# Two half-height matmul pairs in the array: index scores and recurrent gate products on rows 0-63 and 64-127, gate tanh in four pieces

## The chip, the core and the metric

The kernel runs on one core of a Trainium2 chip. The core has a matrix engine (TensorE, PE in the profile, its weight loads PEld), a vector engine (VectorE, DVE), an activation engine (ScalarE, ACT), a general engine (GpSimd, POOL) and a queue engine (SyncE, SP). They run side by side and meet at semaphores. The metric is the device time of one execution in microseconds, the median of several; lower is better.

## What is computed

Two transformer-like blocks run one after the other on 512 tokens of width 1024. Only the first block is touched. Cut to what matters:

```python
u = rms_norm(x, norm1_w) @ w_in                      # split into rnn_x, rnn_gate, q, k, v, iq, ik, iw, g
xc = causal_depthwise_conv(rnn_x, conv_w, conv_b)
r = sigmoid(block_diag_linear(xc, wa, ba))           # 16 blocks of 64 x 64
i = sigmoid(block_diag_linear(xc, wx, bx))
log_a = -8 * r * softplus(-lam); a = exp(log_a)
h = scan(a, sqrt(-expm1(2 * log_a)) * (i * xc))      # recurrence over the tokens
y_rnn = h * gelu(rnn_gate)
rel = relu(einsum('bqhd,bsd->bqhs', iq, ik))         # 8 index heads of 64 channels
score = einsum('bqhs,bqh->bqs', rel, iw) * scale     # its 128 largest per query row are kept
# sparse attention over the kept keys, two output projections, gates, then a feed-forward block
```

After that the first block's feed-forward part follows, and a second block with a gated linear attention, a sliding-window attention, a cross attention and a convolved feed-forward part.

## The kernel before, in words

All activations lie with the channels on the 128 partitions and the 512 tokens along the row. A "job" is one 128-channel output tile of a projection: 8 weight tiles, each with three matmuls (lines 314 to 316: high times high, high times low, low times high part), so 24 matmuls of 512 columns into one PSUM bank. The weights stream in through `raw` (SyncE queue), ScalarE makes the high part (`split`, line 794), GpSimd the low part (line 286), and TensorE takes the job. VectorE takes the result out of PSUM with `take` (a `tensor_tensor` at line 1320). Each engine's order is written out by hand; semaphores carry the dependences.

**Index scores.** The 512 tokens are 4 tiles of 128; for tiles 1 to 3 and 8 heads there are 24 products, of 256, 384 and 512 columns (line 393). Two heads of 64 channels share one 128-partition tile of `p1`. The key tile `ikz` has two copies: `ikz[:, 0]` holds the key in partitions 0-63 and zeros below, `ikz[:, 1]` zeros above and the key in partitions 64-127, so each product runs over all 128 rows and the zeros drop the other head. The zeros are written by a VectorE memset (line 1382). Each product goes to one of three PSUM banks `s_ps[n % 3]`; ScalarE applies relu (line 866) into one of two buffers, and VectorE multiplies by the head's weight and adds (lines 1317 and 1324). TensorE waits before product n for relu n-3, ScalarE before relu n for sum n-2.

**Recurrent part.** Four pairs of tiles (u = 0 and 1), by a loop of three and one pair more (`rnn_pair` on ScalarE and VectorE, `rnn_body` on TensorE). For each tile VectorE finishes the convolution (`conv_tail`), TensorE makes two gate products from it (`rnn_gates`, line 430), over all 128 rows, with a block-diagonal 128 x 128 weight for each gate, into one bank each, and one semaphore step after the second. ScalarE's `rnn_decay` then takes a tanh of each bank (lines 909 and 910), waits for them, and takes an exp and a second tanh (lines 912 and 913). TensorE's order in one round of the loop is: two jobs, gates of tile 0, a job, gates of tile 1, a job. ScalarE's order is: head of the convolution (line 898) and a square (line 903) for each tile, two splits, `rnn_decay(0)`, a split, `rnn_decay(1)`, two tanh for the gelu (line 947), a split, two square roots, two copies to `b_hi`. In the last pair the three later jobs and splits are absent. VectorE uses the two decays one after the other, then the scan (line 1493).

Where names in rows need a word: "score" and "o" are PSUM banks, "job" the two job banks, "turn" the banks `t_ps`, "arena" the large SBUF tile that holds `p1`, `ikz`, `rc`, `rr`, `ri` and most others.

## Time and profile before

| | us |
|---|---|
| median of 3 runs (1743.75 to 1743.93) | 1743.75 |
| the profiled execution | 1743.67 |
| its span, from first to last instruction | 1741.6 |
| TensorE busy in it | 1659.6 |
| VectorE, ScalarE, GpSimd busy | 727.8, 693.1, 791.0 |
| index products on TensorE | 60.0 to 76.4 |
| VectorE's top-128 search | 95.3 to 154.8 |
| recurrent part, first to last gate product | 172.2 to 269.0 |

The 1741.6 us of the span and the 2.1 us around it make the 1743.67 us. The profile shows for each engine what it did, when, and what its idle time ended with. "Idle before" with an arrow names what came last. A product in plain 32-bit format stands in the profile as two matmul records, so "x24" in index rows is 12 products, and a gate visit of two products is four records. The granted clock (PEclk) is the share of the full TensorE clock: 1.00 is 2.4 GHz, 0.50 is 1.2 GHz.

### The profile page before, as it was taken

To read this page: it belongs to the slowest core of one execution; us is meant where nothing else is said; L and a number is where in the kernel's file an instruction comes from. 1 tells how busy PE (TensorE), PEld (TensorE's weight loads), DVE (VectorE), ACT (ScalarE), POOL (GpSimd) and SP (SyncE) were. 2 spreads that over 40 slices of the span, in tenths; PEclk is the share of its full clock that TensorE was granted. 3 is DMA by queue.
4 is the path that set the end of the run, shared out by engine and by line. 5 is a ranking of instruction groups with operands and counts; after the bars stand their busy time and mean duration, and the time that the engine had idled before them with its cause. 6 is when DMAs were issued, how large, how long until landed. Compare 5 with 4: busy or idle time off the path is not lost.

```text
span 1741.6 us, 23147 instructions
## 1 busy us (share of the span) xinstructions
PE 1659.6 (95%) x7686; PEld 1350.5 (78%) x7686; DVE 727.8 (42%) x1343; ACT 693.1 (40%) x1127; POOL 791.0 (45%) x1060
## 2 busy tenths in 40 slices
PE   6999986999999999999999999789999999999997
PEld 5787764777788888888888888678986888888886
DVE  5487886545323321212123532633223453353354
ACT  5322655544333432323233423843354443243242
POOL 5334442222355454545455541035843456456453
PEclk9999998999999999999999999999999999999998
DMA  5122221111222323223233222013421233223221
GB/s 184 59 73 81 76 72 49 49 49 46 99 97 97 97 97 97 97 96 96 96 105 97 73 88 70 1 61 121 143 88 49 85 103 103 92 96 102 94 96 64
DMA packets 45100, 149.64 MB, mean 86 GB/s; under 512 B 4648, under 2 KB 7856, under 8 KB 45040
## 3 DMA queue, kind: packets, MB, share of 16 engines
q1 hardware_dynamic: 38016, 138.43, 24.3%
q10 hardware_dynamic: 7024, 10.41, 1.7%
q8 instruction: 38, 0.62, 0.1%
q14 instruction: 22, 0.18, 0.0%
HBM read 146.58 MB, written 2.11 MB: 85 GB/s over the span
## 4 chain that ended last, share of the span: by engine, by line
PE 86%; DVE 9%; ACT 3%; issue 2%; ACTq 0%; DVEq 0%
PE job L314 24%; PE job L316 24%; PE job L315 24%; DVE arena L1317 2%; PE o L486 2%; PE score L456 2%; DVE arena L1426 1%; DVE small L1423 1%; DVE arena L1320 1%; PE score L393 1%; PE score L430 1%; PE score L714 1%; DVE arena L1493 1%; PE job L746 1%; PE turn L355 1%
## 5 line engine op out<-in xcount | busy, mean ns | idle before, releaser
L286 POOL TENSOR_TENSOR w_lo<-w_raw,w_hi 128x256 fp32r<-128x256 f32 x1056 | 790.8, 781 | 924.5 <-ACT w_hi L794 923.8
L314 PE MATMUL job<-a_hi,w_hi 128*128 128x512 f32 (+1 forms) x1120 | 432.9, 387 | 16.5 <-POOL w_lo L286 9.8
L316 PE MATMUL job<-a_hi,w_lo 128*128 128x512 f32 (+1 forms) x1120 | 424.7, 379 | 0.0
L315 PE MATMUL job<-a_lo,w_hi 128*128 128x512 f32 (+1 forms) x1120 | 424.5, 379 | 0.0
L794 ACT ACTIVATE w_hi<-w_raw 128x1024 fp32r<-128x1024 f32 x264 | 275.2, 1050 | 282.8 <-PE job L316 273.0
L314 PE MATMUL job<-b_hi,w_hi 128*128 128x512 f32 x952 | 374.9, 394 | 0.0
L316 PE MATMUL job<-b_hi,w_lo 128*128 128x512 f32 x952 | 371.0, 390 | 0.0
L315 PE MATMUL job<-b_lo,w_hi 128*128 128x512 f32 x952 | 370.4, 389 | 0.0
L314 PEld LDWEIGHTS job<-a_hi,w_hi 128*128 128x128 f32 x1120 | 212.6, 190 | 59.6 <-DVE a_lo L1317 10.8
L315 PEld LDWEIGHTS job<-a_lo,w_hi 128*128 128x128 f32 x1120 | 212.6, 190 | 39.5 <-issue 2.1
L316 PEld LDWEIGHTS job<-a_hi,w_lo 128*128 128x128 f32 x1120 | 212.0, 189 | 39.8
L316 PEld LDWEIGHTS job<-b_hi,w_lo 128*128 128x128 f32 x952 | 178.7, 188 | 37.7
L314 PEld LDWEIGHTS job<-b_hi,w_hi 128*128 128x128 f32 x952 | 178.8, 188 | 36.6 <-issue 0.2
L315 PEld LDWEIGHTS job<-b_lo,w_hi 128*128 128x128 f32 x952 | 178.9, 188 | 36.0 <-issue 0.2
L1320 DVE TENSOR_TENSOR arena<-arena,job 128x512 f32<-128x512 f32 (+1 forms) x80 | 55.0, 688 | 274.1 <-PE job L316 274.1
L1320 DVE TENSOR_TENSOR arena<-job,rstd 128x512 f32<-128x512 f32 (+1 forms) x117 | 80.1, 688 | 188.1 <-PE job L316 160.4
L1317 DVE SCALAR_TENSOR_TENSOR arena<-arena,vec 128x512 f32<-128x512 f32 x112 | 98.7, 881 | 65.4 <-ACT arena L1267 53.0
L809 ACT ACTIVATE sq<-arena 128x512 f32<-128x512 f32 x48 | 30.2, 631 | 129.5 <-DVE arena L1320 127.2
L1320 DVE TENSOR_TENSOR a_lo<-arena,a_hi 128x512 f32 (+1 forms) x62 | 42.3, 692 | 69.8 <-ACT a_hi L1026 42.2
L1267 ACT ACTIVATE arena<-arena,vec 128x512 f32<-128x512 f32 x44 | 35.6, 808 | 87.8 <-DVE arena L1320 87.8
L1025 ACT ACTIVATE arena<-arena 128x512 f32<-128x512 f32 x32 | 20.2, 632 | 106.5 <-DVE arena L1317 106.5
L1317 DVE SCALAR_TENSOR_TENSOR arena<-job,rstd 128x512 f32<-128x512 f32 x32 | 22.1, 692 | 91.2 <-PE job L316 86.6
(255 smaller groups left out, 1386.7 us busy)
## 6 DMA issues: line engine op xcount, KB each, us to landing
w_raw<-w_all SPq DMA_DIRECT2D x264, 512.0 KB, 3.3
arena<-x_t ACTq DMA_DIRECT2D x8, 512.0 KB, 6.0
out_t<-arena ACTq DMA_DIRECT2D x8, 256.0 KB, 2.1
arena<-rg_w ACTq DMA_DIRECT2D x4, 256.0 KB, 2.7
arena<-row_table ACTq DMA_DIRECT2D x1, 1024.0 KB, 5.2
arena<-mem_t ACTq DMA_DIRECT2D x1, 1024.0 KB, 6.6
arena<-consts ACTq DMA_DIRECT2D x1, 384.0 KB, 3.7
cst<-consts ACTq DMA_DIRECT2D x1, 260.0 KB, 8.1
```

The source lines that it names most:

```text
L286: nc.gpsimd.tensor_tensor(w_lo[:, sl, c], raw[:, sl, c], w_hi[:, sl, c].bitcast(F32), ALU.subtract).then_inc(s("lo_ready"), 1)
L314: mm(ps[:, 0:n], w_hi[:, sl, c], hi[:, kt, 0:n], start=kt == 0, stop=False)
L315: mm(ps[:, 0:n], w_hi[:, sl, c], lo[:, kt, 0:n], start=False, stop=False)
L316: ins = mm(ps[:, 0:n], w_lo[:, sl, c], hi[:, kt, 0:n], start=False, stop=kt == last)
L456: mm(ps, q_now[:, u, qt * P:qt * P + P], kz[:, 2 * kvt + half, 0:w], start=True, stop=True).then_inc(s("att_mm"), 1)
L486: ins = mm(o_ps[:, kt * P:T], vz[:, 2 * kvt + half, kt, :], prob_t[:, kt, kt * P:T], start=half == 0 and kt == 0, stop=half == 1 and kt == ...
L794: fn(w_hi[:, sl], raw[:, sl], ACT.Copy).then_inc(s("hi_ready"), 1)
L809: fn(sq[:, f % 2, :], src, ACT.Square).then_inc(s("sq_ready"), 1)
L1025: fn(act_s[:, c % 2, :], act_t[:, c % 2, :], ACT.Square).then_inc(s("ff_sq"), 1)
L1267: fn(f_c[u], f_u[u][:, PAD:PAD + T], ACT.Identity, scale=vcol("conv_w2", col + 88), bias=vcol("conv_b2", col)).then_inc(s("f_head"), 1)
L1317: return v.scalar_tensor_tensor(out=out_, in0=a, scalar=sc, in1=b, op0=op0, op1=op1)
L1320: return v.tensor_tensor(out_, a, b, op)
```

## The change

- The second key copy moves into the same row as the first: `ik_rows` holds the key in partitions 0-63 and again in 64-127, with no zeros. Head h uses rows 0-63 or 64-127 of both operands, so two consecutive products stand on different halves of the array's rows. The memset of `ikz` is gone.
- The two gate products of a tile work on rows 0-63 and on rows 64-127. The weight tile is 128 x 128 and holds both gates: the first product's bank has gate a of the even block in partitions 0-63 and gate x of the even block in 64-127; the second product's bank has gate x of the odd block in 0-63 and gate a of the odd block in 64-127. The load of these weights is half as large.
- So each tanh reads two banks. It becomes four activations of 64 partitions x 512, two of which read one half of the partitions and write the other.

```diff
-        ikz = tiles(30, 2)
+        ik_rows = arena[:, 30, :]
...
-        rgw = tiles(30, 2)[:, :, 0:2 * P]
+        rgw = tiles(30, 2)[:, :, 0:P]
...
-                mm(s_ps[n % 3][:, 0:P * (t + 1)], p1[:, J_IQ + h // 2, t * P:t * P + P],
-                   ikz[:, h % 2, 0:P * (t + 1)], start=True, stop=True).then_inc(s("idx_mm"), 1)
+                r = slice(64 * (h % 2), 64 * (h % 2) + 64)
+                mm(s_ps[n % 3][:, 0:P * (t + 1)], p1[r, J_IQ + h // 2, t * P:t * P + P],
+                   ik_rows[r, 0:P * (t + 1)], start=True, stop=True).then_inc(s("idx_mm"), 1)
...
                 for c in range(2):
-                    ins = mm(rnn_ps[u][c][:], rgw[:, u, c * P:c * P + P], rc[u], start=True, stop=True)
+                    r = slice(64 * c, 64 * c + 64)
+                    ins = mm(rnn_ps[u][c][:], rgw[r, u, :], rc[u][r, :], start=True, stop=True)
...
-            act.dma_start(ikz[64:128, 1, :], ikz[0:64, 0, :]).then_inc(s("ik_landed"), 16)
+            act.dma_start(ik_rows[64:128, :], ik_rows[0:64, :]).then_inc(s("ik_landed"), 16)
...
-                fn(rr[u], rnn_ps[u][0][:], ACT.Tanh, scale=0.5, bias=half_ba_at(f)).then_inc(s("act_step"), 1)
-                fn(ri[u], rnn_ps[u][1][:], ACT.Tanh, scale=0.5, bias=half_bx_at(f)).then_inc(s("rnn_tanh"), 1)
+                even, odd = slice(0, 64), slice(64, 128)
+                fn(rr[u][even], rnn_ps[u][0][even], ACT.Tanh, scale=0.5, bias=half_ba_at(f)[even]).then_inc(s("act_step"), 1)
+                fn(rr[u][odd], rnn_ps[u][1][odd], ACT.Tanh, scale=0.5, bias=half_ba_at(f)[odd]).then_inc(s("act_step"), 1)
+                fn(ri[u][even], rnn_ps[u][0][odd], ACT.Tanh, scale=0.5, bias=half_bx_at(f)[even]).then_inc(s("act_step"), 1)
+                fn(ri[u][odd], rnn_ps[u][1][even], ACT.Tanh, scale=0.5, bias=half_bx_at(f)[odd]).then_inc(s("rnn_tanh"), 1)
...
-            did(v.memset(ikz, 0.0))
...
-            stt(ikz[0:64, 0, :], p1[0:64, 0, :], vcol("ikn")[0:64], t_ps[0][0:64, :]).then_inc(s("ik_normed"), 1)
+            stt(ik_rows[0:64, :], p1[0:64, 0, :], vcol("ikn")[0:64], t_ps[0][0:64, :]).then_inc(s("ik_normed"), 1)
...
-    rg_w = np.zeros((8, P, 2 * P), f32)
+    rg_w = np.zeros((8, P, P), f32)
...
-        rg_w[n // 2, r, P + 64 * (n % 2):P + 64 * (n % 2) + 64] = wx[n]
+        rg_w[n // 2, r, 64 - 64 * (n % 2):P - 64 * (n % 2)] = wx[n]
```

On VectorE, early in the program, between the set-up of the small columns and the first norm. Before:

```order
L1320 TENSOR_TENSOR small<-vec 128x1
L1380 MEMSET arena 128x2048
L1381 MEMSET arena 128x2048
L1382 MEMSET arena 128x1024
L1339 RECIPROCAL rcol<-rcol 128x4
L1320 TENSOR_TENSOR arena<-job,rstd 128x512 x2
```

And now:

```order
L1325 TENSOR_TENSOR small<-vec 128x1
L1385 MEMSET arena 128x2048
L1386 MEMSET arena 128x2048
L1344 RECIPROCAL rcol<-rcol 128x4
L1325 TENSOR_TENSOR arena<-job,rstd 128x512 x2
```

The third memset is gone; the reciprocal, for which TensorE waits with the spread of the norm (line 355), follows the second.

On ScalarE, `rnn_decay(1)` of the loop: it begins after the split of line 794 and is followed by the gelu's tanh. Before:

```order
L794 ACTIVATE w_hi<-w_raw 128x1024
L908 REGISTER_ALU
L909 REGISTER_ALU
L909 ACTIVATE arena<-score,small 128x512
L910 REGISTER_ALU
L910 ACTIVATE arena<-o,small 128x512
L912 ISA
L912 ACTIVATE arena<-arena,small 128x512
```

And now:

```order
L796 ACTIVATE w_hi<-w_raw 128x1024
L910 REGISTER_ALU
L912 REGISTER_ALU
L912 ACTIVATE arena<-score,small 64x512
L913 ISA
L913 ACTIVATE arena<-o,small 64x512
L914 REGISTER_ALU
L914 ACTIVATE arena<-score,small 64x512
L915 ISA
L915 ACTIVATE arena<-o,small 64x512
L917 ISA
L917 ACTIVATE arena<-arena,small 128x512
```

Nothing moved past anything else; two activations stand where one stood, twice. TensorE has the same instructions in the same order, with 64 instead of 128 rows at lines 393 and 430 (now 394 and 432).

## Rows read from the trace of the kernel before

**Rows 1.** The head of the page.

```profile
span 1741.6 us, 23147 instructions
```

**Rows 2.** Chain of waits at 28 to 34 us: start us, us, what.

```profile
31.81 0.16 issue
31.98 0.91 DVE arena L1382
32.89 0.05 DVE rcol L1339
```

**Rows 3.** Timeline of TensorE: start us, us, what, [idle before <-releaser].

```profile
32.98 1.16 PE L355 MATMUL turn<-cst,rcol 128*128 128x128 f32 x8 [1.51 <-DVE rcol L1339]
```

**Rows 4.** Timeline of VectorE and of ScalarE in the index stage.

```profile
72.06 5.89 DVE L1317 SCALAR_TENSOR_TENSOR arena<-arena,small 128x512 f32<-128x512 f32 x7 [0.24 <-ACT arena L866]
...
76.43 0.60 ACT L866 ACTIVATE arena<-score 128x512 f32<-128x512 f32 x1 [0.26 <-PE score L393]
```

**Rows 5.** Timeline of VectorE after the index stage.

```profile
102.82 0.69 DVE L1320 TENSOR_TENSOR arena<-job,rstd 128x512 f32<-128x512 f32 x1 [1.12 <-PE job L316]
...
158.79 1.29 DVE L1320 TENSOR_TENSOR arena<-job,rstd 128x512 f32<-128x512 f32 x2
```

**Rows 6.** Stretches: busy (count) of PE, PEld, DVE, ACT, POOL, clock, DMA share, GB/s.

```profile
156.60:159.50 2.90, 0.15 (x1) 0.00 (x0) 2.81 (x8) 0.00 (x0) 2.69 (x4) 0.98 0.56 181
159.40:162.80 3.40, 3.26 (x8) 2.58 (x9) 2.53 (x5) 2.28 (x3) 0.76 (x1) 0.50 0.49 154
...
1111.70:1115.00 3.30, 3.30 (x17) 3.30 (x17) 0.90 (x4) 2.98 (x12) 0.00 (x0) 0.50 0.00 0
1120.10:1123.00 2.90, 0.15 (x1) 0.00 (x0) 1.31 (x6) 2.90 (x11) 0.00 (x0) 1.00 0.00 0
...
1142.40:1145.70 3.30, 3.30 (x10) 2.57 (x9) 2.95 (x5) 2.60 (x5) 0.62 (x1) 0.51 0.00 0
```

**Rows 7.** Timeline of TensorE around the gate products of the second pair.

```profile
200.47 3.61 PE L430 MATMUL score<-arena 128*128 128x512 f32 x4 [2.94 <-DVE arena L1317]
...
209.39 1.02 PE L430 MATMUL score<-arena 128*128 128x512 f32 x2
210.24 1.02 PE L430 MATMUL o<-arena 128*128 128x512 f32 x2
```

**Rows 8.** Timeline of ScalarE, second pair and last pair.

```profile
204.18 1.28 ACT L909 ACT_TABLE_LOAD   x1 [0.78 <-PE score L430]
205.47 0.69 ACT L909 ACTIVATE arena<-score,small 128x512 f32<-128x512 f32 x1
206.06 0.68 ACT L910 ACTIVATE arena<-score,small 128x512 f32<-128x512 f32 x1
...
208.32 1.04 ACT L794 ACTIVATE w_hi<-w_raw 128x1024 fp32r<-128x1024 f32 x1
211.39 0.69 ACT L909 ACTIVATE arena<-score,small 128x512 f32<-128x512 f32 x1 [2.03 <-PE o L430]
...
267.07 0.80 ACT L913 ACTIVATE arena<-arena,small 128x512 f32<-128x512 f32 x1
269.19 0.69 ACT L909 ACTIVATE arena<-score,small 128x512 f32<-128x512 f32 x1 [1.32 <-PE o L430]
```

**Rows 9.** Timeline of TensorE where half-height products stand already (line 581).

```profile
1023.51 1.05 PE L564 MATMUL score<-arena 128*128 128x128 f32 x8
1024.49 1.71 PE L581 MATMUL turn<-arena 64*128 64x128 f32 x16
1026.13 0.50 PE L314 MATMUL job<-b_hi,w_hi 128*128 128x512 f32 x1
1026.46 0.40 PE L315 MATMUL job<-b_lo,w_hi 128*128 128x512 f32 x1
```

**Rows 10.** The products of line 581 in two short stretches: length, PE busy (count touched).

```profile
1024.90:1024.93 0.03, 0.03 (x3) 0.03 (x2) 1.00 0.00 0
1025.29:1025.32 0.03, 0.03 (x5) 0.03 (x4) 1.00 0.00 0
```

## Prediction, made before the changed kernel ran

> **What bounds the kernel now.** I read the page first, then the chain of waits, then the timelines of the touched stages, then stretches with the granted clock. The span is 1741.6 us [rows 1], the profiled execution 1743.67, the median 1743.75; the sum below is made against 1743.67 and the difference of 0.08 is ignored. Most of the chain is TensorE's job matmuls, which the change leaves alone, so what counts is the first 286 us. The chain there goes: VectorE's memsets at 30 to 33 us, then TensorE without a pause to 102.6 (the index products are part of it), then VectorE's top-128 search to 158.8, then TensorE's jobs, then four rounds in which it passes through TensorE, ScalarE and VectorE in turn. A gain on TensorE in the index stage reaches the end, since VectorE idles 1.12 us at 102.82 for a job of TensorE's; later in the search it is VectorE alone, which then starts earlier by the same amount [rows 5]. After 286 us everything only moves, unless the clock changes.
>
> **1. The memset of the zero rows.** It takes 0.91 us and stands right ahead of the reciprocal that TensorE waits for [rows 2]. TensorE has idled 1.51 us by then [rows 3], so the cover ends 0.6 us beyond the gain. Gain: 0.91 us, all on the path. Lower bound 0.8 (the issue gap of 0.16 may stay), upper 1.07.
>
> **2. Index products.** Does TensorE overlap products on different row halves? The trace has such products at line 581: 4 products (8 records) on one half, then 8 records on the other. In a slice where one half runs 3 records are in flight, in the slice where the second has begun there are 5 [rows 10]. So yes. The same rows price the change of array shape. The 8 records of line 564 take 0.98 us to the next start; at 0.11 each they need 0.89, so entering costs 0.09. On leaving, the first job matmul takes 0.33 us (1026.13 to 1026.46) instead of 0.23 [rows 9]. With the first half-height weight load not hidden and the drain on the way out, both estimates of mine at 0.1, entering and leaving cost about 0.2 each.
>
> But this stage is mostly VectorE's. In the last third it spends 5.89 us on 7 sums, 0.84 each, idling 0.24 before them; TensorE needs 0.86 for a product of 512 columns (two records of 0.43), and relu waits 0.26 for it [rows 4]. With overlap TensorE drops out and VectorE's 0.84 sets the pace, so the sums end only 0.2 to 0.6 us earlier. TensorE gains more: its last product may start when relu 20 is done, which follows sum 18, five sums before the end: 5 x 0.84 = 4.2 us before the last sum ends, then 0.1 + 0.60 for relu, 0.1, and 0.86 for the product: it ends 2.5 us before the last sum. Before, the last relu starts at 76.43, so the product ended at 76.4, and the last sum ended at 77.95: 1.5 us before. That is 1.0 us earlier, plus 0.2 for VectorE's idling, minus 0.2 for leaving. I take 0.95 us (0.4 to 1.3). The waits stay where they are; queued behind them on TensorE is the V job, which nothing else holds.
>
> **3. Gate products.** At full clock a visit is 4 records of 0.43 = 1.71 us (209.39 to about 211.1); after an idle of 2.94 us the clock is 1.2 GHz and each record takes about 0.86 [rows 7]. Overlapped, a visit takes 0.86 + 0.05 for the second start + 0.2 to enter = 1.1, and 0.2 is lost on leaving. At half clock it is 1.7 + 0.2 against 3.6.
>
> **4. Tanh in four pieces.** No half-height activation stands in the trace. Bounds: an activation's time goes by its columns, so 64 x 512 costs 0.59 us from start to start (205.47 to 206.06), like 128 x 512; at worst it is a full 0.69 with no overlap of successive ones [rows 8]. At the other end, if half the height were half the work, nothing is added. I take 0.59, since all 512 columns remain: two more pieces, +1.18 us per tile (0 to +1.6), 9.4 us of ScalarE time in all. Only what of it lies on the chain counts:
>
> - Pair 0 (no idle ahead, full clock): tile 1's tanh starts when TensorE has done visit, job, visit. Gain 1.71 - 1.3 = 0.4 for the first, 0.6 for the second, against +1.18: **+0.15**.
> - Pairs 1 and 2: ScalarE is free at 203.40 (0.78 before 204.18). Then table load 1.28, the pieces to the end of the split (205.47 to 209.36, 3.89), plus 1.18: tile 1 may start at 209.8 instead of 211.39. ScalarE's idle of 2.03 us is thus used up [rows 8]. TensorE: the first visit is 1.65 shorter, of which the job gives back about half as more of it falls in the low clock, and the second is 0.6 shorter: also about 209.8. So -1.5 + 1.18 = **-0.35** each. ScalarE holds it there even if the clock were full, so the clock matters little here.
> - Pair 3: only 1.32 us of ScalarE's time is idle before tile 1 (267.87 to 269.19). The first tile's two extra pieces use 1.18 of it, so tile 1 starts just 0.15 earlier, however fast TensorE is, and then pays 1.18: **+1.05**.
>
> Sum: 0.15 - 0.7 + 1.05 = +0.5 us. The halved weight load was not waited for: 0. Moving halves across partitions: 0.
>
> A rule of the Trainium skill speaks against this part: TensorEngine Tiling (Array Packing), section Performance Considerations, warns that tiling speeds up TensorE but not the emptying of PSUM, which may become the bottleneck. Taken alone it would say that all eight tiles pay, +9.4 us; the rows of ScalarE's idle time say that three pairs of four hide most of it. The page's section Tiling Modes says that a change of mode drains the array; rows 9 agree, at about 0.1 us for the gap that is seen.
>
> **5. The clock.** TensorE idles at 156.6 to 159.5 and then runs at half clock for 3.4 us, which costs 1.7 us in the jobs that lead to the first gates. Idles of such a length don't always do this: 1120.1 to 1123.0 has the same length, at full clock, and no row shows a fall at it [rows 6]. What decides is where an idle falls, and parts 1 and 2 move this one by 1.86 us. I give 0.55 that the fall goes, 0.45 that it stays. The jobs after it have their weights ready, so the whole 1.7 us would be gained. Later falls, as at 1111.7 and 1142.4 [rows 6], cost 1.2 to 1.7 us each and may also go, and a new one may appear.
>
> **The sum.** -0.9 - 0.95 - 1.7 + 0.5 = -3.05 us: 1743.67 - 3.05 = 1740.6; with a little for a new fall I forecast **1740.8 us**.
>
> **The rivals.**
> - *A, forecast*: the fall at 159.4 goes, others about as before: 1740.8. Chance 0.40; its own range 1739.5 to 1742.
> - *B, the fall stays*, all else as summed: 1743.67 - 1.35 = 1742.3 (up to 1744 if the index gain is at its lower bound). Chance 0.22.
> - *C, the shift also takes one to three later falls away* (1.2 to 1.7 each): 1740.6 - 1.4 to - 4 = 1736.6 to 1739.2. For it: several falls follow idles of 2 to 3 us whose place counts, and nothing reserves their place. Against: some idles that have no fall may get one. Chance 0.28.
> - *D, slower: the gate halves do not overlap.* At line 581 overlap began only after several records of one half; a gate visit has two records a half. If the second half waits for the first, a visit costs 1.71 + 0.4 instead of 1.1 + 0.2. Tile 1 of pairs 0 to 2 then starts 0.8 us later than before, not 1.0 to 1.5 earlier, and pays 1.18: +2.0 x 3, pair 3 +1.5, index gain about 0: 1743.67 + 7.5 - 0.9 = 1750.3. It makes the kernel slower by more than what can be told once pairs 0 to 2 lose over 1.0 us each. Chance 0.06.
> - *E, the pieces cost 0.69 or more apiece* without pipelining across banks and halves: +0.4 for each tile, so +0.8 a pair: A and B become 1744 to 1745.5. Chance 0.04.
> - *The change does not do what it says* (the halves of the index do not overlap, VectorE keeps its pace anyway): part 2 gives 0: inside B.
>
> **How the numbers follow.** A measurement of this kernel can tell about 0.2%, 3.5 us, from no change, so faster means below 1740.3, slower above 1747.2. C is faster wholly (0.28); of A's range about a quarter is (0.09): faster 0.37. D is slower (0.06). The rest, 0.57, is within. The range runs from inside C to E's lower end: 1737.3 to 1744.2; it leaves out D, most of E, and the lowest part of C.
>
> **What would show it.** Memset: the spread of the norm (line 355) starts at 32.1, not 32.98. Index: the V job starts about 1.9 us earlier than 76.4; VectorE's gaps in the last third are gone; the take before the first gates moves from 158.8 to 156.9. Clock: full or half at the jobs behind it. Gates: records of both halves start within 0.1 us of each other. ScalarE: pieces 0.59 apart; its idle before tile 1's pieces is near zero in all pairs but the first; in pair 3 the end of the recurrent part comes 1 us later relative to its start. Wrong if: records of a visit follow one another at 0.43; pieces take under 0.4 or over 0.65; or the falls of the clock change in the part after 300 us by more than two.

## The result: slower by 0.3%, and the profile after

The kernel after takes 1749.26 us (median of 10 runs, 1745.72 to 1752.24), the kernel before 1743.84 us (10 runs, 1742.16 to 1744.78); the ratio is 1.0029, with a 95% interval of 1.0020 to 1.0038. The forecast was 1740.8 us with a range of 1737.3 to 1744.2. The profiled execution of the kernel after took 1751.23 us; its page begins:

```profile
span 1749.4 us, 23174 instructions
```

The span was 1741.6 us before [rows 1]. The table cuts this difference at six places that both traces have; each column is what was added (+) or saved (-) in the stretch that ends there, in us. I worked it out from the start times of the instructions in the traces. The lower rows are kernels from the experiments, on the same footing: each is one execution, compared with the profiled execution of the kernel before. Behind the last column the closing norm takes up to 1.3 us more or less, with the clock that it meets, so a row does not add up to the difference of its times exactly.

| kernel | to the norm's spread (32.98) | to the V job's second matmul (76.46) | to the last top-k step (154.04) | to the first attention turn (285.94) | to the last score product of the next stage (963.22) | to the last job matmul (1726.30) | time of this execution |
|---|---|---|---|---|---|---|---|
| after | -0.84 | +0.09 | 0.0 | **+3.27** | +0.83 | **+4.19** | 1751.23 |
| after, profiled again | -0.90 | -0.16 | 0.0 | +4.03 | +0.96 | +2.31 | 1748.91 |
| index part alone | -0.75 | -0.16 | 0.0 | -0.05 | +0.01 | +1.23 | 1742.68 |
| gate part alone | +0.44 | +0.02 | 0.0 | +3.16 | +0.82 | +2.03 | 1749.17 |
| four pieces, full-height products | +0.45 | +0.01 | 0.0 | +7.37 | +1.28 | -1.71 | 1751.45 |
| half-height products, two tanh | +0.22 | +0.02 | 0.0 | -5.12 | +1.07 | -1.49 | 1738.83 |
| memset moved | -1.02 | +0.04 | 0.0 | -1.18 | +1.30 | -1.65 | 1741.41 |
| memset moved, early signal | +0.25 | -0.08 | 0.0 | -3.14 | +1.13 | -1.54 | 1740.62 |

So the change loses in two places: the recurrent part (154 to 286 us), which holds the gate products and the tanh, and the time behind 963 us, where none of its instructions runs. The first column also holds what differs between executions ahead of the changed code: up to 0.45 us, and 1.3 us in the last row, where TensorE stands at half clock to 32.4 us and the spread waits for TensorE's own jobs. The recurrent part, too, differs between executions where its code is the same: -0.05 (index part alone), -1.18 (memset moved; the fall of the clock at 231.1 us is missing there), and +3.27 against +4.03 in the two of the kernel after.

**The start.** TensorE's timeline in the kernel after (start us, us, what, [idle before <-releaser]):

```profile
32.14 1.16 PE L355 MATMUL turn<-cst,rcol 128*128 128x128 f32 x8 [0.40 <-DVE rcol L1344]
```

The same row stood at 32.98 with 1.51 us of idle [rows 3]. From the start of VectorE's first memset to its reciprocal it is now 3.83 us (28.14 to 31.97) instead of 4.90 (27.91 to 32.81); 0.23 us of the 1.07 are lost to a later start in this execution. The gain of 0.84 us lies within the forecast's 0.8 to 1.07.

**The index stage.** VectorE's sums, ScalarE's last relu and the first V job matmuls of the kernel after, from the timelines of the three engines:

```profile
60.53 0.35 DVE L1329 TENSOR_SCALAR arena<-arena,small 128x256 f32<-128x256 f32 x1 [0.42 <-ACT arena L868]
...
71.97 5.88 DVE L1322 SCALAR_TENSOR_TENSOR arena<-arena,small 128x512 f32<-128x512 f32 x7 [0.24 <-ACT arena L868]
...
76.24 0.60 ACT L868 ACTIVATE arena<-score 128x512 f32<-128x512 f32 x1 [0.25 <-DVE arena L1322]
...
75.37 0.50 PE L314 MATMUL job<-a_hi,w_hi 128*128 128x512 f32 x1
75.71 0.39 PE L315 MATMUL job<-a_lo,w_hi 128*128 128x512 f32 x1
```

The first sum of the stage in the kernel before, VectorE's timeline:

```profile
61.14 0.35 DVE L1324 TENSOR_SCALAR arena<-arena,small 128x256 f32<-128x256 f32 x1 [0.23 <-ACT arena L866]
```

Before, the relu waited 0.26 us for TensorE and the seven sums began at 72.06 [rows 4]. Now the relu waits 0.25 us for VectorE, and the seven sums begin at 71.97, although the first sum of the stage began 0.61 us earlier. Part of that is the fall of the clock at 64.8 us in this one execution. In the kernel with the index part alone (an experiment below), whose execution has no such fall, the rest of the loss sits at one place, the fourth sum. VectorE's timeline there:

```profile
60.61 0.35 DVE L1325 TENSOR_SCALAR arena<-arena,small 128x256 f32<-128x256 f32 x1 [0.42 <-ACT arena L867]
61.06 1.07 DVE L1318 SCALAR_TENSOR_TENSOR arena<-arena,small 128x256 f32<-128x256 f32 x2
62.67 2.84 DVE L1318 SCALAR_TENSOR_TENSOR arena<-arena,small 128x256 f32<-128x256 f32 x5 [0.53 <-DVE arena L1318]
```

The fourth sum starts 2.06 us after the first, against 1.64 in the kernel before.

**A gate visit**, TensorE's timeline:

```profile
208.64 0.69 PE L432 MATMUL score<-arena 64*128 64x512 f32 x1
208.65 0.69 PE L432 MATMUL o<-arena 64*128 64x512 f32 x1
209.17 0.59 PE L432 MATMUL score<-arena 64*128 64x512 f32 x1
209.18 0.59 PE L432 MATMUL o<-arena 64*128 64x512 f32 x1
209.70 0.50 PE L314 MATMUL job<-a_hi,w_hi 128*128 128x512 f32 x1
```

The two job matmuls behind the same visit in the kernel before, whose first record starts at 209.39 [rows 7]:

```profile
210.70 0.79 PE L314 MATMUL job<-a_hi,w_hi 128*128 128x512 f32 x1
211.33 0.40 PE L315 MATMUL job<-a_lo,w_hi 128*128 128x512 f32 x1
```

Both halves start within 0.01 us of each other. From the first of them to the next job's first matmul it is 1.06 us and to its second 1.39 (210.03), against 1.31 and 1.94 before. So a visit is 0.55 us shorter, with the price of entering and leaving in it; the prediction had 0.4, or 0.6 without the price of leaving. The prediction's 1.71 is four records of 0.43, which is not the distance to the next job.

**The tanh pieces** of the second pair, ScalarE's timeline, and below them rows up to its tile 1 and two rows of the last pair:

```profile
204.60 0.69 ACT L912 ACTIVATE arena<-score,small 64x512 f32<-64x512 f32 x1
205.32 0.69 ACT L913 ACTIVATE arena<-score,small 64x512 f32<-64x512 f32 x1
206.03 0.69 ACT L914 ACTIVATE arena<-score,small 64x512 f32<-64x512 f32 x1
206.74 0.68 ACT L915 ACTIVATE arena<-score,small 64x512 f32<-64x512 f32 x1
207.57 0.82 ACT L917 ACTIVATE arena<-arena,small 128x512 f32<-128x512 f32 x1
...
209.00 1.04 ACT L796 ACTIVATE w_hi<-w_raw 128x1024 fp32r<-128x1024 f32 x1
209.94 0.67 ACT L912 ACTIVATE arena<-score,small 64x512 f32<-64x512 f32 x1
...
269.49 0.80 ACT L918 ACTIVATE arena<-arena,small 128x512 f32<-128x512 f32 x1
270.19 0.67 ACT L912 ACTIVATE arena<-score,small 64x512 f32<-64x512 f32 x1
```

The pieces start 0.71 us apart, where the two full-height ones of before were 0.59 apart (205.47, 206.06 [rows 8]): a tile needs 2.97 us from its first tanh to its Exp. The idle of 2.03 us ahead of tile 1 is gone, as foretold: ScalarE goes from the split at 209.00 straight on. In the last pair it goes straight from L918 to the next tile.

**The clock**, in stretches of the kernel after (length, busy (count) of PE, PEld, DVE, ACT, POOL, then the granted clock, DMA share, GB/s):

```profile
64.90:68.10 3.20, 3.20 (x10) 2.27 (x10) 2.52 (x5) 2.31 (x5) 0.00 (x0) 0.50 0.00 0
160.40:163.60 3.20, 3.20 (x9) 2.49 (x8) 2.01 (x3) 0.82 (x1) 2.31 (x3) 0.50 0.30 116
...
228.70:235.30 6.60, 4.68 (x10) 2.65 (x11) 5.63 (x7) 4.30 (x6) 5.56 (x7) 0.50 0.26 74
...
1136.60:1146.70 10.10, 8.21 (x35) 7.51 (x35) 0.14 (x1) 3.80 (x10) 0.00 (x0) 0.50 0.00 0
1150.30:1153.50 3.20, 3.20 (x9) 2.52 (x8) 2.54 (x5) 2.20 (x4) 0.93 (x2) 0.50 0.00 0
```

The fall at 160 us is still there. The one at 228.7 lasts 6.8 us instead of 3.4, and the next, from 259.3 on, 17.1 instead of 6.8. At 1136.6 the clock is at 1.2 GHz for 10 us, and once more at 1150.3 for 3.4 us. The kernel before had full clock there up to its fall of 3.4 us at 1142.4 [rows 6]:

```profile
1136.60:1142.30 5.70, 2.85 (x20) 2.52 (x20) 1.86 (x4) 3.75 (x8) 0.00 (x0) 1.00 0.00 0
```

### The profile page after: what moved, and what is told of

Read it like the earlier page. It is cut to its first block, busy times and chain, and to the rows that moved or that the text cites. A ratio compares the mean times of both kernels' runs of the same rounds, so it can differ in the third digit from the quotient of the medians.

```text
span 1749.4 us, 23174 instructions
## 1 busy us (share of the span) xinstructions
PE 1661.5 (95%) x7686; PEld 1351.1 (77%) x7686; DVE 725.8 (41%) x1342; ACT 704.6 (40%) x1143; POOL 791.3 (45%) x1060
## 4 chain that ended last, share of the span: by engine, by line
PE 85%; DVE 8%; ACT 4%; issue 2%; ACTq 0%; DVEq 0%
PE job L314 24%; PE job L316 24%; PE job L315 24%; PE o L488 2%; DVE arena L1322 2%; PE score L458 2%; DVE arena L1430 1%; DVE small L1427 1%; DVE arena L1325 1%; PE score L394 1%; PE score L716 1%; DVE arena L1497 1%; PE job L748 1%; PE turn L355 1%; ACT arena L1166 1%
```

## Experiments

### The two parts apart

The first pair of kernels splits the change. The index part alone takes the half-height index products, the single `ik_rows` tile and the missing memset, and leaves the gates:

```diff
-                mm(s_ps[n % 3][:, 0:P * (t + 1)], p1[:, J_IQ + h // 2, t * P:t * P + P],
-                   ikz[:, h % 2, 0:P * (t + 1)], start=True, stop=True)
+                r = slice(64 * (h % 2), 64 * (h % 2) + 64)
+                mm(s_ps[n % 3][:, 0:P * (t + 1)], p1[r, J_IQ + h // 2, t * P:t * P + P],
+                   ik_rows[r, 0:P * (t + 1)], start=True, stop=True)
...
-            did(v.memset(ikz, 0.0))
```

> Index part of the change alone: half-height index products and no memset of zero rows; gates and tanh as before. By the sum of parts as the two traces now show them, the spread of the norm starts 0.85 us earlier, the index stage itself gives back 0.1 (its sums go at VectorE's pace), and the top-128 search ends 0.75 us earlier: 1743.8 - 0.75 = 1743.1 if nothing else moves. Theory 'half-height products count as less work for the clock': the granted clock falls inside the index stage (near 64 to 68 us) as in the changed kernel, though TensorE is busy. Rival 'it was the gates': no fall there. Theory 'alignment': the falls after 1080 us differ from before in number or length, and the total is off the 1743.1 by 1 to 4 us with nothing changed there.

Measured: 1743.2 us (median of 11, 1740.47 to 1746.3), ratio 0.9998 (0.9989 to 1.0007). In its profiled execution the start gives 0.75 us and the index stage 0.16; behind 963 us the clock takes 1.23 and, in the closing norm, gives back 1.3 (its product of line 355 at 1730.80 takes 1.16 us instead of 2.07). There is no fall of the clock at 64 to 68 us, and the falls behind 1080 us differ (6.8 us at 1134.7), as its last theory had it. The gate part alone is the rest of the change:

```diff
-                    ins = mm(rnn_ps[u][c][:], rgw[:, u, c * P:c * P + P], rc[u], start=True, stop=True)
+                    r = slice(64 * c, 64 * c + 64)
+                    ins = mm(rnn_ps[u][c][:], rgw[r, u, :], rc[u][r, :], start=True, stop=True)
```

together with the smaller weight load and the four tanh pieces.

> Gates part alone: half-height gate products, half weight load, four tanh pieces; index stage and memset as before. Theory 'pieces': ScalarE's pieces of 0.71 us from start to start cost more than TensorE's 1.1 us visits give back; the attention stage starts about 3.5 to 4 us later than before, total 1747.5 to 1748 if later falls are as before. Rival 'the index part is what hurts': total within 1.5 us of before.

Measured: 1748.8 us (5 runs, 1748.47 to 1751.06), ratio 1.0035 (1.0021 to 1.0049). It loses 3.16 us in the recurrent part, as expected (the attention starts 3.6 us later), and 2.03 behind 963 us. The loss of the kernel after comes with the gate part.

### ScalarE's price and TensorE's gain apart

The kernel before with the tanh in four half-height pieces, each reading and writing the same rows, over full-height products (the cuts from here on leave out the signals at the ends of some lines, and this one the two lines that are replaced):

```diff
+                fn(rr[u][even], rnn_ps[u][0][even], ACT.Tanh, scale=0.5, bias=half_ba_at(f)[even])
+                fn(rr[u][odd], rnn_ps[u][0][odd], ACT.Tanh, scale=0.5, bias=half_ba_at(f)[odd])
+                fn(ri[u][even], rnn_ps[u][1][even], ACT.Tanh, scale=0.5, bias=half_bx_at(f)[even])
+                fn(ri[u][odd], rnn_ps[u][1][odd], ACT.Tanh, scale=0.5, bias=half_bx_at(f)[odd])
```

> Kernel before with only the tanh split: four pieces of 64 partitions, each reading and writing the same half, full-height gate products. Separates the pieces from TensorE's gain. If a piece is 0.71 from start to start because of its half height or its change of half, two more pieces add 1.4 us a tile: pair 0 +1.4, pairs 1 and 2 +1.4 each (ScalarE's idle of 2.0 hides the first tile's), pair 3 +1.4 + 0.1: attention starts 5.8 us later, total near 1749.6. If the 0.71 came from reading one half and writing the other, pieces are 0.59 apart here and the total is 4.7 us later, 1748.5.

Measured: 1753.07 us (5 runs, 1751.45 to 1753.73), ratio 1.0057 (1.0043 to 1.0070). The recurrent part is 7.37 us longer, which is more than the 5.8 expected. By pairs, each from the end of the one before to its second copy to `b_hi`, it is 1.55, 2.41, 1.53 and 1.92 us; 0.9 of the second goes with a fall of the clock at 200.8 us that lasts 6.8 instead of 3.4 us in this execution. ScalarE's timeline shows the same step without any crossing of rows between input and output:

```profile
207.60 0.69 ACT L910 ACTIVATE arena<-score,small 64x512 f32<-64x512 f32 x1
208.31 0.69 ACT L911 ACTIVATE arena<-score,small 64x512 f32<-64x512 f32 x1
209.03 0.68 ACT L912 ACTIVATE arena<-score,small 64x512 f32<-64x512 f32 x1
209.74 0.69 ACT L913 ACTIVATE arena<-score,small 64x512 f32<-64x512 f32 x1
```

The other side is the kernel before with half-height gate products and two full-height tanh (which leaves the gates of odd and even heads mixed up):

```diff
-                    ins = mm(rnn_ps[u][c][:], rgw[:, u, c * P:c * P + P], rc[u], start=True, stop=True)
+                    r = slice(64 * c, 64 * c + 64)
+                    ins = mm(rnn_ps[u][c][:], rgw[r, u, :], rc[u][r, :], start=True, stop=True)
```

> The kernel before with the gate products on half the rows each (and the weight load of half the size), but the tanh left as it was, two of 128 x 512 per tile; the gates of odd and even heads are thus mixed up. It prices what TensorE alone gives. Theory (the products give back what the pieces lose): tile 1's tanh starts 1.0 us earlier against its pair in pair 0 and about 1.5 in pairs 1 and 2, where ScalarE would be free earlier; pair 3 gains 0.1 (its ScalarE has only 1.32 us idle before tile 1) to 1.3. The end of the recurrent part comes 3.5 to 5 us earlier than in the kernel before, the time is 1739 to 1741. Rival (the clock takes the gain away: the overlapped products keep TensorE busy for a shorter time, and the two falls at 230 to 290 us get longer, as they did in the kernel after, 6.8 and 17.1 us in place of 3.4 and 6.8): the gain per pair falls to 0 to 0.5 us from pair 2 on, the end of the recurrent part comes at most 2 us earlier, and the time is within 0.1% of before.

Measured: 1738.69 us (9 runs, 1737.49 to 1742.65), ratio 0.9973 (0.9964 to 0.9983). The recurrent part is 5.12 us shorter, a little more than the first theory said, and by pairs 1.20, 1.34, 1.39 and 1.31; the rival, that the clock takes it away, falls. The two alone add up to 7.37 - 5.12 = +2.25; together they measured +3.16 to +4.03 (gate part alone; after in its two executions). The change bought 5.1 us on TensorE and paid 6.5 to 7.4 us on ScalarE for it, the lower figure without the longer fall.

### What makes a piece cost 0.71

The kernel after with its pieces in another order, so that the first two write rows 0 to 63 and the last two rows 64 to 127:

```diff
                 fn(rr[u][even], rnn_ps[u][0][even], ACT.Tanh, scale=0.5, bias=half_ba_at(f)[even])
-                fn(rr[u][odd], rnn_ps[u][1][odd], ACT.Tanh, scale=0.5, bias=half_ba_at(f)[odd])
                 fn(ri[u][even], rnn_ps[u][0][odd], ACT.Tanh, scale=0.5, bias=half_bx_at(f)[even])
                 fn(ri[u][odd], rnn_ps[u][1][even], ACT.Tanh, scale=0.5, bias=half_bx_at(f)[odd])
+                fn(rr[u][odd], rnn_ps[u][1][odd], ACT.Tanh, scale=0.5, bias=half_ba_at(f)[odd])
```

> The kernel after, with the four tanh pieces of a tile in another order: even half of rr, even half of ri, odd half of ri, odd half of rr. In the kernel after every piece writes another half or another buffer than the one ahead in the same way as it reads it; here the first two write the same rows (0 to 63) and the last two the same rows (64 to 127). The pieces of the kernel after start 0.71 us apart (204.60, 205.32, 206.03, 206.74), where 128 x 512 pieces of before started 0.59 to 0.60 apart. Theory 1, the spacing belongs to a change of the rows that are written or of the PSUM bank: here the steps inside a pair of like rows come down to about 0.60 and a tile's four starts to the Exp take 2.86 - 0.22 = about 2.6 us. Theory 2, it belongs to the half height itself: all starts stay 0.71 apart, 2.9 us per tile. Time by either within 0.1% of the kernel after (1749): the look is for the spacing.

Measured: 1749.78 us (one run), recurrent part +4.76, with a fall at 199.2 us that lasts 6.8 us. All steps stay at 0.71 (204.27, 204.98, 205.69, 206.39). Taken alone this spoke for the half height itself. But here every piece still reads other rows of PSUM than the one ahead. So one more order, over full-height products, in which reading and writing change rows together, and only between the second and the third piece:

```diff
+                fn(rr[u][even], rnn_ps[u][0][even], ACT.Tanh, scale=0.5, bias=half_ba_at(f)[even])
+                fn(ri[u][even], rnn_ps[u][1][even], ACT.Tanh, scale=0.5, bias=half_bx_at(f)[even])
+                fn(rr[u][odd], rnn_ps[u][0][odd], ACT.Tanh, scale=0.5, bias=half_ba_at(f)[odd])
+                fn(ri[u][odd], rnn_ps[u][1][odd], ACT.Tanh, scale=0.5, bias=half_bx_at(f)[odd])
```

> The kernel before (full-height products) with the four tanh pieces in the order even half of rr, even half of ri, odd half of rr, odd half of ri, each reading the rows that it writes. The step from the first to the second piece is thus the step from rr to ri of the kernel before (another bank, another buffer, the same first row), which took 0.59, in all but the height. Theory 1, half height itself makes the step 0.71: 0.71 here too, in all three steps. Theory 2, it is the change of rows: the first and the third step are 0.59 to 0.60, the second 0.71. Time 1752 to 1754, like the other run with pieces on full-height products, less 1 to 2 us if theory 2 holds.

Measured: 1752.98 us (one run), recurrent part +6.66 instead of +7.37. Of the 6.66, 1.4 us lie ahead of the first pair, where a fall at 161.9 us lasts 6.8 us; the four pairs take 5.28 us more, instead of 7.41. ScalarE's timeline:

```profile
211.17 0.69 ACT L910 ACTIVATE arena<-score,small 64x512 f32<-64x512 f32 x1
211.76 0.67 ACT L911 ACTIVATE arena<-score,small 64x512 f32<-64x512 f32 x1
212.46 0.69 ACT L912 ACTIVATE arena<-score,small 64x512 f32<-64x512 f32 x1
213.04 0.67 ACT L913 ACTIVATE arena<-score,small 64x512 f32<-64x512 f32 x1
```

Steps of 0.59, 0.70, 0.58. A half-height activation takes as long as a full one, and 0.12 us more where it reads or writes other rows than the one ahead of it. The three orders cover the cases: in the one above a change of the read rows alone is enough (first step of the reordered kernel), in the kernel after a change of the written rows alone (its second to third piece, both of which read rows 64 to 127). In the changed kernel's data flow each piece has its own pair of rows read and rows written, so no order of the four escapes.

### Moving the memset, and a signal for each product

What of the gain is to be had without the pieces? First the kernel before with the memset of the zero rows behind the reciprocal:

```diff
+            dve.wait_ge(s("norm_root"), 1)
+            v.reciprocal(rcol[:, :, 0], rcol[:, :, 0]).then_inc(s("norm_inv"), 1)
             did(v.memset(ikz, 0.0))
-            norm_inverse(1)
+            dve.wait_ge(s("rstd_ready"), 1)
```

> Kernel before with the memset of the zero rows moved behind the reciprocal that TensorE waits for, into VectorE's wait for the norm; nothing else. Sum of parts: -0.85 us at the spread of the norm, kept to the end of the search and of the recurrent part: 1743.0. Theory 'alignment': a pure shift of 0.85 us also changes the falls of the clock later on, so the total differs from 1743.0 by a fall's 1.2 to 1.7 us in one direction or the other.

Measured: 1741.45 us (11 runs, 1740.52 to 1745.31), ratio 0.9993 (0.9984 to 1.0002). The spread starts 1.02 us earlier, for 0.85 expected. The whole gain of the change's index part is there with full-height products. The 1.18 us in the recurrent part are the clock's: nothing was changed there, and the interval of the ratio holds 1. Then, on top of it, full-height gate products that each give their own signal, so that the first tanh starts beside the second product:

```diff
-                    ins = mm(rnn_ps[u][c][:], rgw[:, u, c * P:c * P + P], rc[u], start=True, stop=True)
-                ins.then_inc(s("rnn_mm"), 1)
+                    mm(rnn_ps[u][c][:], rgw[:, u, c * P:c * P + P], rc[u], start=True, stop=True).then_inc(s("rnn_mm"), 1)
...
-                act.wait_ge(s("rnn_mm"), n)
+                act.wait_ge(s("rnn_mm"), i * 4 + (2 * u + 1))
                 fn(rr[u], rnn_ps[u][0][:], ACT.Tanh, scale=0.5, bias=half_ba_at(f))
+                act.wait_ge(s("rnn_mm"), i * 4 + (2 * u + 2))
```

> The kernel before with the memset of the zero rows moved behind the reciprocal (as in the earlier run), and with a signal of its own for each of the two full-height gate products of a tile: the first tanh waits for the first product alone, the second for the second. Nothing is computed differently. Theory: the change tried to bring tile 1's tanh forward by 0.6 us or more with overlapped products; half of that is to be had without any cost for ScalarE, since a product of two records ends 0.86 us (1.7 at 1.2 GHz) before its partner. ScalarE's idle before tile 1 shrinks by 0.6 to 0.9 us in each pair, limited by the second tanh, which may start when it started before less 0 (it now waits for its product at 0.1 behind the first tanh's end at most): per pair a gain of 0.5, 2 us in all, and with the memset's 0.9 a time of 1740 to 1741.5. Rival: the gain is taken by the clock (a fall longer or one more later): then the end of the recurrent part is 2 to 3 us earlier in span but the time is 1742 to 1744.

Measured: 1740.39 us (11 runs, 1737.69 to 1741.42), ratio 0.9978 (0.9969 to 0.9987): **faster than the kernel before, by 0.2%, and than the kernel after**. ScalarE's timeline ahead of tile 1 of the second pair:

```profile
209.75 0.69 ACT L908 ACTIVATE arena<-score,small 128x512 f32<-128x512 f32 x1 [0.28 <-PE score L430]
210.60 0.69 ACT L910 ACTIVATE arena<-o,small 128x512 f32<-128x512 f32 x1 [0.17 <-PE o L430]
```

The idle of 2.03 us [rows 8] is down to 0.28 + 0.17, without a single instruction more on ScalarE. This pair is a lucky one: the fall of the clock at 200.4 us is missing in this execution. At the same place in the first and third pair, where the clock is as before, the idle is 1.60 for 2.05 and 1.95 for 2.44 us.

By pairs the recurrent part is 0.58, 2.17, 0.63 and 1.03 us shorter, against 0.5 expected for each; a longer fall at 158.9 us takes 1.3 back ahead of them, which makes the 3.14 of the table. What the signal is worth is thus about 0.6 us a pair where the clock is alike. The medians of the kernels with the memset alone and with both are 1.06 us apart, where 2 were expected, and their intervals overlap slightly.

### Quarter products and two full-height tanh

Two kernels cut each gate product once more, so that both heads' results land in their own rows of one bank and two full-height tanh are enough. The weight tile holds a and x of a head side by side. A product of 4 columns ahead carries the wait. Both have the memset moved; the second has a signal for each pair:

```diff
+                mm(rnn_ps[u][0][:, 0:4], rgw[:, u, :], rc[u][:, 0:4], start=True, stop=True)
                 for c in range(2):
-                    ins = mm(rnn_ps[u][c][:], rgw[:, u, c * P:c * P + P], rc[u], start=True, stop=True)
+                    for k in range(2):
+                        r, o = slice(64 * k, 64 * k + 64), slice(64 * c, 64 * c + 64)
+                        ins = mm(rnn_ps[u][c][r, :], rgw[r, u, o], rc[u][r, :], start=True, stop=True)
```

> The kernel before with the memset moved behind the reciprocal, and each gate product cut into two of 64 rows x 64 columns of the array, so that odd and even heads land in their own halves of one bank and the tanh stays two activations of 128 x 512 per tile, nothing being mixed up. A full-height product of 4 columns stands ahead of the four and carries the wait. Theory: the four 64 x 64 products run side by side as the two halves did; a visit takes 1.1 us and 0.2 to 0.3 for the small product ahead, instead of 1.71. Then most of the gain of the half-height products without the pieces (5.1 us at the end of the recurrent part) is had: 3.5 to 5 us there, and a time of 1737.5 to 1740. Rival 1: only products on different rows overlap, those on different columns of the same rows follow one another: a visit takes 1.71 + 0.4 us, the recurrent part ends 1 to 3 us later than with the memset moved alone, 1742.5 to 1744.5. Rival 2: none of the four overlaps: a visit of 3.4 us, 1752 or more.

> The 64 x 64 products with a signal behind each pair of them (a's two, x's two), so that the first tanh need not wait for x. Theory: if all four run side by side they end together and the signal of a comes at most 0.1 us before x's: within 1 us of the run without it. If only products on different rows overlap (rival 1 there), a's pair is done 0.86 us before x's, and this kernel is 2 to 4 us faster than that one: 1739 to 1741.

Measured: 1745.21 us (11 runs, 1738.3 to 1747.62), ratio 1.0005 (0.9995 to 1.0016), and 1744.21 us (11 runs, 1742.01 to 1747.13), ratio 1.0005 (0.9996 to 1.0014). A visit in the second kernel, TensorE's timeline:

```profile
207.82 0.28 PE L429 MATMUL score<-arena 128*128 128x4 f32 x2
208.03 1.07 PE L433 MATMUL score<-arena 64*64 64x512 f32 x4
208.94 1.02 PE L433 MATMUL o<-arena 64*64 64x512 f32 x4
209.90 0.50 PE L314 MATMUL job<-a_hi,w_hi 128*128 128x512 f32 x1
```

The two products of one gate (four records) overlap, the two gates follow one another: 0.21 + 0.91 + 0.96 = 2.08 us to the next job, against 1.31 in the kernel before. This looks like the first rival of the first expectation (the median lies a little above its 1742.5 to 1744.5), but its reason is not tested: these kernels have no products on other columns of the same rows. The product of gate x reads rows 64k to 64k+63 and writes the same rows of its bank (`rnn_ps[u][c][r, :]`), just as that of gate a does; only the place of the weights in the tile differs. The Trainium skill, TensorEngine Tiling (Array Packing), section Tiling Modes, counts four independent tiles of 64 x 64, each tied to the partitions that it reads and writes. By that, the four products here use two of the four tiles, twice each, and the trace agrees, with two at a time (208.03 and 208.94). Whether all four tiles would run side by side, with x written to the other half of its bank, no run here shows.

The second kernel's expectation missed: the early signal was to bring 2 to 4 us, the medians differ by 1.0, and the profiled recurrent part is 1.35 us longer than without. The clock hides the signal's worth: in pairs 0 and 2 the first kernel is 0.72 and 0.69 us slower than the kernel before, the second 0.15 and 0.12; the first kernel's other two pairs were 0.88 and 1.14 us faster, where falls were missing or shorter. As the two medians lie near the time of the kernel before (1743.85), the quarter products throw away what the moved memset gave.

### Does half height alone change the clock in the index stage

The fall at 64.9 us in the kernel after raised the question whether half-height products bring such a fall. The kernel before with every index product on rows 0 to 63, so that none can overlap:

```diff
-                mm(s_ps[n % 3][:, 0:P * (t + 1)], p1[:, J_IQ + h // 2, t * P:t * P + P],
-                   ikz[:, h % 2, 0:P * (t + 1)], start=True, stop=True)
+                mm(s_ps[n % 3][:, 0:P * (t + 1)], p1[0:64, J_IQ + h // 2, t * P:t * P + P],
+                   ikz[0:64, 0, 0:P * (t + 1)], start=True, stop=True)
```

> The kernel before with all 24 index products on rows 0 to 63 (odd heads are computed from the even head's rows, so those scores are wrong); the memset stays. TensorE gets as many columns and as many records as before, but none of them can overlap, and each uses half of the rows. The question is the fall of the clock at 64.8 to 68.2 us in the kernel after, inside the index stage, which neither the kernel before nor the kernel with the index part alone shows. Theory 1, half the rows count less with the chip's clock: the granted clock falls to 0.50 inside the index stage (59 to 77 us) here too. Theory 2, only idle time counts, and TensorE is as busy as before: no fall in this stage. The index stage as a whole: VectorE's sums keep 0.84 us each, so the V job starts at 76.4 to 76.9 as before.

Measured: 1744.14 us (one run). In the stretch of the index stage the granted clock is full:

```profile
65.70:69.00 3.30, 3.30 (x12) 1.88 (x11) 2.79 (x6) 2.49 (x6) 0.00 (x0) 1.00 0.00 0
```

This execution has no fall in the stage. Of the five executions with half-height index products (this one, the kernel after twice, the index part alone and the kernel after with its pieces reordered) one has it, of the eleven with full-height products none. So half height does not bring the fall regularly; whether it makes it likelier is open. The V job starts 0.41 us later against the spread, which is more than expected: the price of entering and leaving half height (0.2 on VectorE's first wait, 0.2 from the last product to the second job matmul), with no overlap to pay for it.

### The loss behind 963 us

Two kernels are the kernel before with needless memsets on VectorE between the recurrent part and the attention, four and two of them, so that the rest of the program starts later; the third is the kernel after, profiled again:

```diff
             rnn_pair(3, False)
+            for _ in range(4):
+                did(v.memset(ikz, 0.0))
+                settle()
```

> The kernel before with four needless memsets of 0.9 to 1.0 us on VectorE between the recurrent part and the attention (3.6 to 4.0 us in all); everything after them starts that much later against the start of the program, as it does in the kernel after (+3.4 us), and nothing else is changed. In the kernel after, and in the two other kernels with half-height gates and four pieces, 4 us more are lost behind 963 us, most of it where the granted clock is 0.50 for 10.3 us from 1136 or 1137 us on (3.4 us in the kernel before). Theory 1, that long fall comes with the later start alone: here too the clock is 0.50 for about 10 us at 1136 to 1147, and the time is before + 3.8 + 2 to 4 = 1749.5 to 1752. Theory 2, it has another cause in the changed code: no such fall, at most 6.8 us at 1146, and the time is before + 3.8 less up to 1 us: 1746.8 to 1748.

> The same with two memsets: 1.8 to 2.0 us later. Theory 1: the stretch of half clock behind 1130 us has again another length than in the kernel before (3.4 us) and than with four memsets, somewhere from 3.4 to 10.3 us; the time may be anywhere from before + 1 to before + 6. Theory 2: 3.4 us as before, time before + 1.9 = 1745.7.

> The kernel after, profiled a second time. Which of its falls of the clock belong to the kernel and which to one execution? Those in the recurrent part (228.6 to 235.4 and 259.3 to 276.4 us) and the one of 10.3 us at 1136.5 come again within 2 us of their places, if they belong to the kernel; the one inside the index stage (64.8 to 68.2 us), which no other kernel with the index part showed, does not come again. Time 1747 to 1752 as in its other runs.

Measured: 1748.73 us (6 runs, 1744.81 to 1751.13), ratio 1.0031 (1.0019 to 1.0044) with four; 1747.94 us (one run) with two; 1748.91 us for the kernel after again. In the profiled execution with four memsets two falls of the recurrent part were shorter or missing, so that the point at 963 us is only 1.40 us later than before and the long fall does not come; with two it is 3.47 us later, by chance almost as in the kernel after (3.36). Stretches of the kernel with four, then of the one with two, then two of the second execution of the kernel after:

```profile
1137.00:1142.00 5.00, 2.83 (x24) 2.40 (x22) 0.15 (x1) 2.45 (x5) 0.00 (x0) 1.00 0.00 0
```

```profile
1137.00:1147.00 10.00, 8.20 (x35) 7.51 (x35) 0.00 (x0) 3.70 (x8) 0.00 (x0) 0.50 0.00 0
```

```profile
64.90:68.10 3.20, 3.20 (x12) 1.43 (x12) 2.74 (x5) 2.57 (x6) 0.00 (x0) 1.00 0.00 0
...
1137.40:1147.40 10.00, 8.20 (x35) 7.51 (x35) 0.00 (x0) 3.70 (x9) 0.00 (x0) 0.50 0.00 0
```

None of the changed code is in the kernel with two memsets, and it has the long fall of the kernel after, and loses 2.1 us there. So theory 1 holds in this execution, with a correction: what counts is how much later the part behind 963 us starts in that execution, not how many memsets stand ahead. Over all 16 profiled executions of this study: where that point lies 3.8 us earlier to 1.4 us later than before (8 executions beside the one of before), the rest of the program takes 1.65 us less to 1.23 us more; where it lies 3.4 to 4.6 us later (after in both executions, gate part alone, reordered pieces, two memsets), the clock is 0.50 for 10 us at 1137, and the rest takes 2.0 to 4.2 us more; at 9.1 and 9.5 us later (the two kernels with pieces on full-height products) it is -1.71 and +0.86. In the kernel after, all of the 4.19 us arises between 1048 and 1170 us. The fall at 1150.3 us, which its second execution does not have, goes with the difference between 4.19 and 2.31. Where the long fall loses its time shows in TensorE's timeline, before and then after:

```profile
1134.01 1.83 PE L686 MATMUL job<-arena 128*128 128x128 f32 x14 [3.39 <-ACT arena L1181]
1137.29 1.83 PE L686 MATMUL job<-arena 128*128 128x128 f32 x14 [0.69 <-ACT arena L1181]
```

```profile
1137.72 3.36 PE L688 MATMUL job<-arena 128*128 128x128 f32 x14 [4.28 <-ACT arena L1186]
1143.26 3.35 PE L688 MATMUL job<-arena 128*128 128x128 f32 x14 [0.69 <-ACT arena L1186]
```

The same 14 products take 1.83 us at full and 3.36 at half clock. The runs of the kernel with four memsets fall into two groups, 1744.8 to 1745.0 and 1747.1 to 1751.1, as this would have it; only one of the first group was traced. The second execution also answers for the index stage: the fall at 64.9 us is not there again, so it belonged to one execution; the long ones at 229, 260 and 1137 us came again.

## Why the prediction was wrong, step by step

- **1, the memset: right.** 0.91 us forecast; 0.84 and 0.90 in the two executions of the kernel after, and 1.02 where it was only moved.
- **2, the index products: the mechanism was half seen.** TensorE gains on VectorE nearly as the working had it: its last record starts 3.00 us before the last sum ends, against 2.15, so 0.85 for 1.0; and leaving half height costs the 0.2 forecast (0.86 us from that record to the second job matmul, for 0.66). The step that failed is "so the sums end only 0.2 to 0.6 us earlier", with its "plus 0.2 for VectorE's idling". Against the spread they end 0.5 us later: 0.23 since the first one waits for a product behind the change of the array's shape, and 0.27 at the fourth sum (17.08 us from the first to the end of the last in the second execution of the kernel after and with the index part alone, 16.81 before; 17.32 with the fall at 64.8). Why the fourth sum comes late no run shows; it does so only where the halves overlap. From there on the steady pace is 0.86 us a round in both kernels: a relu waits for a sum and the sum for a relu, whoever multiplies. 0.85 - 0.5 - 0.2 leaves 0.15 to 0.16 of 0.95 us in three executions, and -0.09 with the fall at 64.8. The rival that this part gives nothing was nearly the true one.
- **3, the gate products: right.** 1.06 us for 1.1, and the halves start 0.01 apart, so rival D's condition is not met. Alone, with two tanh, they give 5.12 us.
- **4, the tanh pieces: the term that was mis-sized.** 0.59 between pieces became 0.71, which is rival E; from a tile's first tanh to its Exp it is 2.97 instead of 1.42 us (206.89 - 205.47), +1.52 to +1.55 instead of +1.18. That is also the prediction's own sign of being wrong, pieces over 0.65. The bounds did hold it (0 to 1.6), the chance of 0.04 for E did not do it justice: the trace had no piece of that kind, and 0.59 was taken from activations that all used the same rows. By pairs: pair 0 gives +0.42 for +0.15; pair 1 +0.19 for -0.35 (tile 1 starts 1.34 us earlier against its pair, for 1.5); pair 2 +0.80 for -0.35 (only 0.76 earlier: ScalarE idles 0.56 us for TensorE, which the fall at 228.6, twice as long, keeps at half clock, so "the clock matters little here" did not hold); pair 3 +1.65 for +1.05. That is 3.06 for 0.5: of the 2.56 between them, 4 x 0.35 = 1.4 is the piece's price in the four second tiles, about 0.3 the same in the first tile of pair 3, 0.7 the clock in pair 2, and 0.15 a smaller gain in pair 1. The idle ahead of tile 1 went as foretold in the other pairs. In the second execution a fall at 198.6 us lasts 6.8 us as well, and pair 1 gives +1.53. The rule of the Trainium skill that the prediction weighed (TensorEngine Tiling (Array Packing), section PSUM Bottleneck: tiling does not speed up the emptying of PSUM) is borne out here: the tanh that empties a bank takes as long at half height, and cutting it in pieces alone costs 7.37 us, more than the products give.
- **5, the clock: wrong.** The fall at 159.4 was to go with chance 0.55, for 1.7 us. It stayed in the kernel after (160.3) and came again in its second execution (157.7); of the 16 executions just two lack it, both with quarter products, and there the first gate product comes 1.5 us earlier against the search, so its price was about right. A shift of 0.7 us did not move it away. The forecast of 1740.8 rested on its going; rival B, in which it stays, had 0.22, although part 5 gives 0.45 for that, and A and C, which both need it gone, have 0.68 together for its 0.55.
- **What had no term:** that a later start of the rest of the program has a price of its own. The prediction let falls behind 300 us only vanish (rival C) or appear one at a time. B with E's price was 1745.5 at most. As measured, the profiled execution is -0.84 + 0.09 + 3.27 + 0.83 + 4.19 = +7.54 us. The prediction had -0.9, -0.95, -1.7 and +0.5 for the first 286 us, and nothing but 0.2 behind them. The 0.83 in the attention go with half clock that lasts to 293.4 instead of 289.1 us, the 4.19 with the falls at 1136.6 and 1150.3. Without what lies behind 963 us the time would have been 1747.0, which is still outside the range: the mechanism on ScalarE and the fall that did not go away are enough for that.

Not settled is why the clock's long fall at 1137 us belongs to a start 3.4 to 4.6 us later. That a later start is enough is shown by one execution of code that is otherwise that of before, and four more with changed code agree; how the chip decides is not shown.

## What to carry to other kernels

A faster producer is worth nothing by itself where its consumer must do more instructions for it: price the emptying of the result first, in the engine that has no idle left (here pair 3), and with a row of the very form, since a half-height activation costs a full one and more where rows change. Ask what the shorter product was to bring, here an earlier first tanh, and whether a signal placed earlier gives something of it for nothing: with the memset moved it gave 3.4 us where the change lost 5.4. And a few microseconds gained or lost ahead of a stage with idle gaps may be multiplied or swallowed by the clock behind it; compare the stages one by one before believing in the total.

## What the hardware showed that was not expected

- A half-height activation of 512 columns: 0.69 us long, as a full one; 0.59 to the next start on the same rows, 0.71 where the rows read or written change.
- Products on the two row halves start 0.01 us apart even as the very first two on a visit. So do two of 64 x 64 that write the two halves of one bank (208.03 and 208.04); four of them, on the same rows and partitions twice, take 1.87 us to the next job.
- A first product behind a change of shape comes 0.2 us later (0.42 of waiting on VectorE for 0.23), and from the last half-height record to the second job matmul it is 0.86 us, where it is 0.66 behind a full-height one.
- The kernel before, with two memsets more ahead of the attention, reaches the point at 963 us 3.5 us later and has half clock for 10 us at 1137 us, where without them it has full clock; where it reaches that point 1.4 us later, it has full clock too.
